# A differential attention head's two maps merged on VectorE ahead of their turning

## The chip, the cores and the metric

One core of a Trainium2 chip runs the whole program in one launch. The metric is the device time of an execution in microseconds, lower is better. The kernel before was run three times.

## What is computed

Two stacks of layers follow each other on 256 latent tokens of width 1024, with 256 context tokens beside them: an even layer (convolution, neighbourhood attention, SwiGLU), an odd layer (window attention and differential attention, then a mixture of 8 experts), and a second model with two more layers. All data are float32. The change lies in the odd layer's differential attention. It has 4 heads. Each has two sets of queries and keys of width 64 and one set of values of width 128:

```
def joint_softmax(parts, extra=None):
    m = parts[0].max(-1, keepdims=True)
    for p in parts[1:]:
        m = jnp.maximum(m, p.max(-1, keepdims=True))
    ...
    es = [jnp.exp(p - m) for p in parts]
    ...
    return [e / den for e in es]

def diff_attend(q, kvs, lam):
    scale = q.shape[-1] ** -0.5
    ss = [jnp.einsum('bhiqd,bhikd->bhiqk', q, k, preferred_element_type=jnp.float32) * scale for k, _ in kvs]
    ps = joint_softmax(ss)
    out = None
    for p, (_, v) in zip(ps, kvs):
        a = (p[:, :, 0] - lam * p[:, :, 1]).astype(v.dtype)
        o = jnp.einsum('bhqk,bhkd->bhqd', a, v)
        out = o if out is None else out + o
    return out
```

Both maps of a head run over the 512 keys of latent and context tokens. The result of a head goes through an RMS norm of its own and then into the output projection.

## The kernel before

The program is written out by hand for each engine; semaphores order the engines against each other, and the position of an instruction in an engine's own program is its order. An attention is a list of items. An item is one softmax map of 128 queries by 512 keys (by fewer in the even and the second model's attentions). For item i these steps follow each other:

- TensorE, `scores`: queries by keys into the PSUM bank `SC[i % 2]` (L1432). A window item adds a mask (L1434).
- VectorE, in `attn_dve`: the negated maximum of each row into `negm` (L1485 and L1486 with a floor for window items, L1488 without).
- ScalarE, `attn_act`: the exponential into `prob[i % 2]` in SBUF, with the row sums into `den` (L1504).
- TensorE: four 128x128 transposes by the identity into the PSUM bank `PT[i % 2]` (L1460). This is the turning of the map.
- VectorE, `take`: the copy of the turned map into `probT[i % 2]` (L1479).
- TensorE, `outputs`: four matmuls of the turned map by the values into the item's PSUM bank (L1445), the product.

TensorE's order is: scores of item i+1, turning of item i, product of item i-1, then what `aside` adds. Two buffers stand at each place, so the scores of item i+1 wait for the exponential of item i-1, and the exponential of item i waits for the turning of item i-2. The names `sem("scores")`, `max_done`, `exp_done`, `prob_turned`, `probT_done` and `out_ready` count these steps, one for an item. `e.link` makes VectorE wait for the end of its own instruction before the next; `e.put` names an instruction and `e.after` waits for a name.

The odd layer's list is `W_ITEMS + D_ITEMS`: 16 window items (0 to 15), then 16 differential items (16 to 31). `diff_items` orders the latter by head, then map, then block of 128 queries:

```
for hd in range(4):
    for i in range(2):
        for t in range(NT):
```

Between the steps of an item VectorE does other work that `odd_every_dve` hangs on item numbers: the arguments of the window heads' sinks at item 16, the window heads' outputs at 17 (`window_out_dve`, L2136 to L2143), their cut into a high and a low part for the projection at 25 and 28 (`cut_x`, L1362 and L1363), and for the first two differential heads the reciprocals and lambda (`diff_shares_dve`), the scaling of both maps' products (`diff_scale_dve`, L2217), their sum (`diff_add_dve`, L2224) and the sums of squares (`diff_squares_dve`, L2229 and L2230) at 26 to 31. The other two heads follow behind the attention in `diff_out_dve`. On TensorE `odd_aside_pe` turns the window outputs at items 20 and 22 (L2158), and ScalarE copies them out two items later (L2173). Behind the attention TensorE goes on with the output projection (L422, L423, L426): a first block of weights, the turning of the first two differential heads' outputs (L2260), a second block, the turning of the other two, and the rest.

Of the kernel before, what the change touches and what calls it, by code (L numbers as in the profile page):

```python
# [20 lines left out]
P = 128  # L21
TOK = 256
# [113 lines left out]
def program(nc, a, out, plan):  # L136
# [1280 lines left out]
    def attn_pe(e, base, items, ready, *deps, turn=None, aside=None):  # L1417

        e.after(*deps)
        last = len(items)  # L1420

# [15 lines left out]
        def outputs(i):  # L1437
            it = items[i]

            e.eng.wait_ge(sem("probT_done"), base + i + 1)  # L1440
            if it.get("o_free"):
                it["o_free"](e)
            kt = it["n"] // P
            for k in range(kt):
                ins = nc.tensor.matmul(it["o"], probT[i % 2][:, k * P:k * P + P], it["v"][k],  # L1445
                                       start=k == 0, stop=k == kt - 1)
            ins.then_inc(sem("out_ready"), 1)

        scores(0)
        for i in range(last):  # L1450
            if i + 1 < last:
                scores(i + 1)

            e.eng.wait_ge(sem("exp_done"), base + i + 1)
            if i >= 2:
                e.eng.wait_ge(sem("probT_done"), base + i - 1)
            if turn:
                turn(e, i)
            for k in range(items[i]["n"] // P):
                ins = nc.tensor.transpose(PT[i % 2][:, k * P:k * P + P], prob[i % 2][:, k * P:k * P + P], ident)  # L1460
            ins.then_inc(sem("prob_turned"), 1)
            if i >= 1:
                outputs(i - 1)
            if aside:
                aside(e, i)
        outputs(last - 1)

    def attn_dve(e, base, items, floor, *deps, every=None):


        e.after(*deps)

        def take(i):

            e.eng.wait_ge(sem("prob_turned"), base + i + 1)
            if i >= 2:
                e.eng.wait_ge(sem("out_ready"), base + i - 1)
            n = items[i]["n"]
            nc.vector.tensor_copy(probT[i % 2][:, 0:n], PT[i % 2][:, 0:n]).then_inc(sem("probT_done"), 1)  # L1479

        for i, it in enumerate(items):
# [8 lines left out]
            if i >= 1:  # L1490
                take(i - 1)
            if every:
                every(i)
        take(len(items) - 1)

    def attn_act(e, base, items, also=None):
        for i, it in enumerate(items):
# [3 lines left out]
            if i >= 2:  # L1501

                e.eng.wait_ge(sem("prob_turned"), base + i - 1)
# [332 lines left out]
    def diff_items():  # L1836
        items = []
        for hd in range(4):
            for i in range(2):
                for t in range(NT):  # L1840
                    half = slice(i * HD, i * HD + HD)
                    v = [pl[:, t_, 1792 + hd * P:1792 + hd * P + P] for t_ in range(NT)] + \
                        [pc[:, t_, 768 + hd * P:768 + hd * P + P] for t_ in range(NT)]
                    items.append(dict(n=2 * TOK, q=qTo[half, 4 + hd, t * P:t * P + P], k=kTo[half, 2 + hd, :],
                                                    adds=[], v=v, o=psum[4 + hd // 2 * 2 + t][:, (2 * (hd % 2) + i) * P:(2 * (hd % 2) + i) * P + P]))
        items[0]["o_free"] = lambda e: e.after("att_w:o")
        return items

# [302 lines left out]
    def odd_aside_pe(e, i):  # L2151

        if i in W_TURNS:
            b = W_TURNS.index(i)
            for k in range(2):
                for t in range(NT):
                    at, c = (2 * b + k) * P, k * TOK + t * P
                    ins = nc.tensor.transpose(PT[(i - 1) % 2][:, c:c + P], hc[:, t, at:at + P], ident)  # L2158
            e.put(ins, f"att_w:oT_ps{b}")

    def odd_turn_pe(e, i):

        if i - 1 in W_TURNS:
            e.after(f"att_w:oT{W_TURNS.index(i - 1)}")

    def odd_also_act(e, i):
# [3 lines left out]
        if i - 2 in W_TURNS:  # L2170
            b = W_TURNS.index(i - 2)
            e.after(f"att_w:oT_ps{b}")
            e.put(nc.scalar.activation(xf[:, 2 * b:2 * b + 2, :].rearrange("p k t -> p (k t)"), PT[(i - 3) % 2][:, :],  # L2173
                                       ACT.Copy), f"att_w:oT{b}")

    def odd_every_dve(e, base):

        def every(i):
            if i == W_END:
                window_sinks_dve(e, base)  # L2180
            if i == W_END + 1:
                window_out_dve(e, base)
            if i in (25, 28):
                cut_x(e, "cat_o", (i // 28,), lambda b: f"att_w:oT{b}")
            if i in (26, 27):
                if i == 26:
# [6 lines left out]
        return every  # L2193

# [4 lines left out]
    def diff_shares_dve(e, base, half):  # L2199

        e.eng.wait_ge(sem("out_ready"), base + D_HALF + 8 * half)
        e.eng.wait_ge(sem("exp_done"), base + D_HALF + 8 * half)
        if half == 0:
            e.after("lam exp")
            e.link(nc.vector.tensor_tensor(lame[:, 0:1], lame[:, 2:3], lame[:, 3:4], ALU.subtract))
            e.link(nc.vector.tensor_scalar(lame[:, 0:1], lame[:, 0:1], -1.0, -LAM_INIT, ALU.mult, ALU.add))
        own = den[:, W_END + 8 * half:W_END + 8 * half + 8]
        e.link(nc.vector.reciprocal(own, own))
        r = own.rearrange("p (h i t) -> p h i t", i=2, t=NT)
        e.link(nc.vector.tensor_scalar(r[:, :, 1, :], r[:, :, 1, :], lame[:, 0:1], None, ALU.mult))  # L2210

    def diff_scale_dve(e, half, t):

        r = den[:, W_END + 8 * half:W_END + 8 * half + 8].rearrange("p (h i t) -> p h i t", i=2, t=NT)
        for i, to in enumerate((diff_head(half, t), diff_other[half][:, t * 2 * P:t * 2 * P + 2 * P])):
# [1729 lines left out]
```

## Time and profile before

| | us |
|---|---|
| runs, median (lowest to highest) | 2788.96 (2783.48 to 2789.22) |
| profiled execution, span | 2787.6 |
| TensorE busy in the span | 2662.0 |
| VectorE, ScalarE, GpSimd busy | 1838.2, 1445.3, 182.9 |

The page gives the profiled execution by its span alone. The median of the runs is 1.4 us above it and the fastest run 4.1 below it. All times within the trace count from the start of the span. The odd layer's attention lies between 850 and 943 us, the differential items from 901. In the clock column 1.00 is TensorE's full 2.4 GHz and 0.50 is 1.2 GHz. A matmul's length in the timeline holds its way through the array, so that starts, and not lengths, tell how fast one follows another.

### The profile page before, as it was taken

The page shows a single profiled execution, that of the slowest core. Times are in us where ns is not written, and L with a number is a line of the kernel's source. Part 1 is how long each engine was busy: PE and PEld are TensorE (multiplying, and loading weights), DVE is VectorE, ACT ScalarE, POOL GpSimd, SP SyncE. Part 2 cuts the span into 40 slices and gives each one's busy share as a digit, 9 for nine tenths or more (in the row PEclk, how much of TensorE's full clock was granted, in tenths as well). Part 3 has the DMA queues.
Part 4 walks back from the last instruction along what each step waited for, and adds up shares of the span by engine and source line. Part 5 has one row for each costly group of instructions (what it writes and reads, how often), then busy time and mean ns, then how long its engine had stood idle before and what let it go on. Part 6 is the DMA issues. An engine that isn't in the chain of part 4 may idle for free.

```text
span 2787.6 us, 33943 instructions
## 1 busy us (share of the span) xinstructions
PE 2662.0 (95%) x12949; PEld 2210.6 (79%) x12949; DVE 1838.2 (66%) x2324; ACT 1445.3 (52%) x2055; POOL 182.9 (7%) x226
## 2 busy tenths in 40 slices
PE   7999899999999889999999899998999999998998
PEld 5777678888886678888888788887788788777787
DVE  6676677787776655557888656588656556546555
ACT  6563354544453344446777445664445545553553
POOL 2011000000050000000000000002100100100100
PEclk9999999999999989999999999999999999999999
DMA  8673166776660056557999546540364655650444
GB/s 299 226 249 117 61 220 233 242 263 225 227 186 31 1 174 199 186 186 257 326 326 329 195 155 222 157 151 1 119 199 166 203 174 178 205 188 4 158 159 143
DMA packets 260767, 511.40 MB, mean 183 GB/s; under 512 B 9769, under 2 KB 40705, under 8 KB 260496
## 3 DMA queue, kind: packets, MB, share of 16 engines
q1 hardware_dynamic: 256576, 498.11, 53.4%
q0 software_dynamic: 4048, 11.36, 1.4%
q8 instruction: 93, 1.52, 0.2%
q14 instruction: 50, 0.41, 0.0%
HBM read 507.33 MB, written 1.05 MB: 182 GB/s over the span
## 4 chain that ended last, share of the span: by engine, by line
PE 86%; DVE 7%; ACT 3%; DMA 2%; issue 2%; POOL 1%; SPq 0%; DVEq 0%; ACTq 0%; POOLq 0%
PE bank L422 23%; PE bank L423 23%; PE bank L426 23%; PE bank L1432 2%; PE bank L1445 2%; DVE h_hid L2856 1%; PE bank L393 1%; PE bank L1460 1%; PE bank L394 1%; PE bank L395 1%; DVE wlo L330 1%; ACT whi L326 1%; PE bank L541 1%; PE bank L1434 1%; PE bank L2420 1%
## 5 line engine op out<-in xcount | busy, mean ns | idle before, releaser
L330 DVE TENSOR_TENSOR wlo<-raw,whi 128x1024 fp32r<-128x1024 f32 (+1 forms) x964 | 1142.9, 1201 | 662.0 <-ACT whi L326 655.8
L326 ACT ACTIVATE whi<-raw 128x1024 fp32r<-128x1024 f32 (+1 forms) x964 | 986.9, 1035 | 782.8 <-PE bank L426 733.7
L422 PE MATMUL bank<-whi,xhi 128*128 128x512 f32 (+2 forms) x2320 | 884.7, 381 | 22.1 <-issue 12.7
L426 PE MATMUL bank<-whi,xlo 128*128 128x512 f32 (+2 forms) x2320 | 874.8, 377 | 0.0
L423 PE MATMUL bank<-wlo,xhi 128*128 128x512 f32 (+2 forms) x2320 | 874.0, 377 | 0.0
L422 PEld LDWEIGHTS bank<-whi,xhi 128*128 128x128 f32 x2320 | 439.6, 190 | 103.1 <-issue 20.3
L426 PEld LDWEIGHTS bank<-whi,xlo 128*128 128x128 f32 x2320 | 438.9, 189 | 77.2
L423 PEld LDWEIGHTS bank<-wlo,xhi 128*128 128x128 f32 x2320 | 439.9, 190 | 74.5 <-issue 0.5
L422 PE MATMUL bank<-whi,f_hhi 128*128 128x512 f32 x496 | 194.0, 391 | 0.0
L426 PE MATMUL bank<-whi,f_hlo 128*128 128x512 f32 x496 | 193.1, 389 | 0.0
L423 PE MATMUL bank<-wlo,f_hhi 128*128 128x512 f32 x496 | 193.1, 389 | 0.0
L1504 ACT ACTIVATE tmp<-bank,negm 128x512 f32<-128x512 f32 (+2 forms) x112 | 60.8, 543 | 135.2 <-DVE negm L1488 101.2
L426 PEld LDWEIGHTS bank<-whi,f_hlo 128*128 128x128 f32 x496 | 93.1, 188 | 19.4
L423 PEld LDWEIGHTS bank<-wlo,f_hhi 128*128 128x128 f32 x496 | 93.2, 188 | 19.0
L422 PEld LDWEIGHTS bank<-whi,f_hhi 128*128 128x128 f32 x496 | 93.1, 188 | 19.0
L422 PE MATMUL bank<-whi,m_hhi 128*128 128x512 f32 x242 | 95.7, 396 | 0.0
L426 PE MATMUL bank<-whi,m_hlo 128*128 128x512 f32 x242 | 94.6, 391 | 0.0
L423 PE MATMUL bank<-wlo,m_hhi 128*128 128x512 f32 x242 | 94.4, 390 | 0.0
L641 DVE TENSOR_TENSOR f_hlo<-bank,f_hhi 128x512 fp32r<-128x512 f32 (+1 forms) x66 | 42.8, 687 | 72.2 <-ACT f_hhi L597 72.0
L597 ACT ACTIVATE f_hhi<-bank 128x512 fp32r<-128x512 f32 (+1 forms) x66 | 36.2, 595 | 82.9 <-PE bank L541 82.9
L1488 DVE TENSOR_REDUCE negm<-bank 128x1 f32<-128x256 f32 (+2 forms) x96 | 45.9, 479 | 49.7 <-PE bank L1434 31.8
L1460 PE MATMUL bank<-kb,tmp 128*128 128x128 f32 x296 | 55.9, 291 | 13.3 <-ACT tmp L1504 11.9
(574 smaller groups left out, 2804.2 us busy)
## 6 DMA issues: line engine op xcount, KB each, us to landing
raw<-in_ffn_w SPq DMA_DIRECT2D x180, 1024.0 KB, 5.1
raw<-in_moe_w SPq DMA_DIRECT2D x96, 1024.0 KB, 6.1
raw<-in_moe_w SPq DMA_DIRECT2D x48, 768.0 KB, 4.6
raw<-in_ada_w SPq DMA_DIRECT2D x24, 1024.0 KB, 5.6
raw<-in_ev_w_in SPq DMA_DIRECT2D x24, 1024.0 KB, 5.6
raw<-in_ffn_w SPq DMA_DIRECT2D x36, 512.0 KB, 3.6
raw<-in_hyb_w_in SPq DMA_DIRECT2D x18, 1024.0 KB, 5.1
raw<-in_attn_w_qkv SPq DMA_DIRECT2D x18, 1024.0 KB, 5.0
```

The source lines that it names most:

```text
L326: nc.scalar.activation(whole, part, ACT.Copy).then_inc(sem("w_hi"), 1)
L330: nc.vector.tensor_tensor(wlo[s][:, 0:rows, 0:n], part, whole.bitcast(F32), ALU.subtract)\
L422: nc.tensor.matmul(bank[:, 0:n], xk_h, whi[s][:, wk, 0:n], start=first, stop=False)
L423: ins = nc.tensor.matmul(bank[:, 0:n], xk_h, wlo[s][:, wk, 0:n], start=False, stop=last and xl is None)
L426: ins = nc.tensor.matmul(bank[:, 0:n], xk_l, whi[s][:, wk, 0:n], start=False, stop=last)
L597: ins = nc.scalar.activation(hhi[:, at, :].rearrange("p k t -> p (k t)"), T[b // TOK][:, 0:k * TOK], ACT.Copy)
L641: ins = nc.vector.tensor_tensor(hlo[:, at, :].rearrange(flat), T[b // TOK][:, 0:k * TOK], hhi[:, at, :].bitcast(F32).rearrange(flat), ALU. ...
L1432: nc_last = nc.tensor.matmul(bank[:, 0:n], it["q"], it["k"], start=True, stop=not adds)
L1445: ins = nc.tensor.matmul(it["o"], probT[i % 2][:, k * P:k * P + P], it["v"][k], start=k == 0, stop=k == kt - 1)
L1460: ins = nc.tensor.transpose(PT[i % 2][:, k * P:k * P + P], prob[i % 2][:, k * P:k * P + P], ident)
L1488: nc.vector.tensor_reduce(col, SC[i % 2][:, 0:it["n"]], AX.X, ALU.max, negate=True)\
L1504: nc.scalar.activation(prob[i % 2][:, 0:it["n"]], SC[i % 2][:, 0:it["n"]], ACT.Exp, bias=negm[:, i:i + 1], accum_out=den[:, i:i + 1]).then ...
```

## The change

The two maps of a head and block of queries now follow each other: the first is called `lead`, the second `pair`. VectorE merges them before they are turned: the second map is multiplied by c = -lambda x (sum of the first) / (sum of the second), and the first is added. One turning, one copy and one product serve both. The sum of the first map divides the product at the end, as before. `turned_items` numbers the items that are turned, and the banks `PT` and buffers `probT` alternate by this number, which starts at `tb`; in the odd layer 24 of 32 items are turned. The products of four heads and two blocks take two PSUM banks in place of four. The window outputs are turned into banks 6 and 7, so `odd_turn_pe` goes.

```
     def attn_pe(...)
+        def turn_over(i):
+            u = place[i]
+            if items[i].get("pair"):
+                e.after(f"merged{i}")
+            else:
+                e.eng.wait_ge(sem("exp_done"), base + i + 1)
+            if u >= 2:
+                e.eng.wait_ge(sem("probT_done"), tb + u - 1)
...
+            for k in range(items[i]["n"] // P):
+                ins = nc.tensor.transpose(PT[u % 2][:, k * P:k * P + P], prob[i % 2][:, k * P:k * P + P], ident)
+            ins.then_inc(sem("prob_turned"), 1)
...
+            now = i
+            if items[i].get("lead"):
+                now = i - 1 if i and items[i - 1].get("pair") else None
+            elif items[i].get("pair"):
+                now = "later"
+            if now != "later":
+                if now is not None:
+                    turn_over(now)
+                if waiting is not None:
+                    outputs(waiting)
+                waiting = now
     def attn_dve(...)
             if i >= 1:
-                take(i - 1)
+                former = items[i - 1]
+                if former.get("pair"):
+                    former["merge"](e, i - 1)
+                elif not former.get("lead"):
+                    take(i - 1)
+                elif i >= 2 and items[i - 2].get("pair"):
+                    take(i - 2)
     def attn_act(...)
             if i >= 2:
-
-                e.eng.wait_ge(sem("prob_turned"), base + i - 1)
+                if items[i - 2].get("lead"):
+
+                    e.after(f"merged{i - 1}")
+                else:
+                    e.eng.wait_ge(sem("prob_turned"), tb + place[i - 2] + 1)
+    def diff_merge_dve(e, i):
+
+        e.eng.wait_ge(sem("exp_done"), ATT0[2] + i + 1)
+        c = vtop[:, (i - W_END) // 2:(i - W_END) // 2 + 1]
+        e.link(nc.vector.reciprocal(c, den[:, i:i + 1]))
+        e.link(nc.vector.scalar_tensor_tensor(out=c, in0=c, scalar=lame[:, 0:1], in1=den[:, i - 1:i],
+                                              op0=ALU.mult, op1=ALU.mult))
+        own, other = prob[(i - 1) % 2], prob[i % 2]
+        e.put(nc.vector.scalar_tensor_tensor(out=other[:, :], in0=other[:, :], scalar=c, in1=own[:, :],
+                                             op0=ALU.mult, op1=ALU.add), f"merged{i}")
     odd_aside_pe
         if i in W_TURNS:
             b = W_TURNS.index(i)
+            e.after("att_w:o")
...
     odd_every_dve
             if i == W_END:
                 window_sinks_dve(e, base)
+                lambda_total_dve(e)
...
-            if i in (25, 28):
-                cut_x(e, "cat_o", (i // 28,), lambda b: f"att_w:oT{b}")
-            if i in (26, 27):
-                if i == 26:
+            if i in (25, 27):
+                cut_x(e, "cat_o", (i // 27,), lambda b: f"att_w:oT{b}")
+            if i in (28, 29):
+                if i == 28:
                     diff_shares_dve(e, base, 0)
-                diff_scale_dve(e, 0, i - 26)
-            if i == 29:
-                diff_add_dve(e, 0)
+                diff_scale_dve(e, 0, i - 28)
```

`diff_scale_dve` scales one product for a block in place of two, `diff_add_dve` goes in both halves, and `diff_shares_dve` no longer computes lambda, which `lambda_total_dve` does at item 16 with the same two instructions. In the second model's attention only the numbers change (`TURNED4 = 56`).

How the order moves. On TensorE, in the differential part of the odd attention, a little over two items before (o_kT is the keys, `kb` the identity, tmp the maps and turned maps, o_pl and o_pc the values of latent and context):

```order
L1432 MATMUL bank<-o_kT,o_qT 128x512
L1460 MATMUL bank<-kb,tmp 128x128 x4
L1445 MATMUL bank<-o_pl,tmp 128x128 x2
L1445 MATMUL bank<-o_pc,tmp 128x128 x2
L1432 MATMUL bank<-o_kT,o_qT 128x512
```

and now a little over one pair:

```order
L1438 MATMUL bank<-o_kT,o_qT 128x512 x2
L1466 MATMUL bank<-kb,tmp 128x128 x4
L1451 MATMUL bank<-o_pl,tmp 128x128 x2
L1451 MATMUL bank<-o_pc,tmp 128x128 x2
L1438 MATMUL bank<-o_kT,o_qT 128x512 x2
```

A turning and a product stood behind the scores of each item; now they stand behind the scores of two. The turning is that of the pair before, the product that of the pair before it.

On VectorE, from the maximum of item 17 over the window heads' outputs to item 18, before:

```order
L1488 TENSOR_REDUCE negm<-bank 128x1
L1479 COPY tmp<-bank 128x512
L2136 TENSOR_TENSOR den<-den,sinke 128x16
L2137 RECIPROCAL den<-den 128x16
L2143 TENSOR_TENSOR hc<-bank,den 128x256 x4
L1488 TENSOR_REDUCE negm<-bank 128x1
```

and now:

```order
L1517 TENSOR_REDUCE negm<-bank 128x1
L2195 TENSOR_TENSOR den<-den,sinke 128x16
L2196 RECIPROCAL den<-den 128x16
L2202 TENSOR_TENSOR hc<-bank,den 128x256 x4
L1517 TENSOR_REDUCE negm<-bank 128x1
L1901 RECIPROCAL vtop<-den 128x1
L1902 SCALAR_TENSOR_TENSOR vtop<-vtop,few,den 128x1
L1905 SCALAR_TENSOR_TENSOR tmp<-tmp,vtop 128x512
L1517 TENSOR_REDUCE negm<-bank 128x1
L1508 COPY tmp<-bank 128x512
```

Behind the maximum of item 17 stood the copy of item 16; item 16 now has none. Behind the maximum of item 18 stands the first merge (L1901, L1902, L1905), and behind that of item 19 the copy of the merged map.

At the end of the attention on VectorE, before:

```order
L2229 TENSOR_TENSOR y<-hc 128x256
L2230 TENSOR_REDUCE ss<-y 128x2
L1488 TENSOR_REDUCE negm<-bank 128x1
L1479 COPY tmp<-bank 128x512
L2229 TENSOR_TENSOR y<-hc 128x256
L2230 TENSOR_REDUCE ss<-y 128x2
L1479 COPY tmp<-bank 128x512
```

and now:

```order
L2274 TENSOR_TENSOR y<-hc 128x256
L2275 TENSOR_REDUCE ss<-y 128x2
L1517 TENSOR_REDUCE negm<-bank 128x1
L1508 COPY tmp<-bank 128x512
L2274 TENSOR_TENSOR y<-hc 128x256
L2275 TENSOR_REDUCE ss<-y 128x2
L1901 RECIPROCAL vtop<-den 128x1
L1902 SCALAR_TENSOR_TENSOR vtop<-vtop,few,den 128x1
L1905 SCALAR_TENSOR_TENSOR tmp<-tmp,vtop 128x512
L1508 COPY tmp<-bank 128x512
```

The last merge stands behind both rounds of squares, and the last copy directly behind that merge.

## Rows read from the trace of the kernel before

**Rows 1.** Page, parts 1 and 4: busy time, and the chain that ended last.
```profile
PE 2662.0 (95%) x12949; PEld 2210.6 (79%) x12949; DVE 1838.2 (66%) x2324; ACT 1445.3 (52%) x2055; POOL 182.9 (7%) x226
...
PE 86%; DVE 7%; ACT 3%; DMA 2%; issue 2%; POOL 1%; SPq 0%; DVEq 0%; ACTq 0%; POOLq 0%
```

**Rows 2.** Windows: start:end, length, busy PE, PEld, DVE, ACT, POOL, granted clock, DMA share, GB/s.
```profile
899.40:942.20 42.80, 41.99 (x243) 28.30 (x242) 29.93 (x58) 13.77 (x35) 0.61 (x2) 1.00 0.00 1
```

**Rows 3.** Timeline, TensorE, maps 16 and 17: start, length, instruction group.
```profile
900.84 1.12 PE L1432 MATMUL bank<-o_kT,o_qT 64*128 64x512 f32 x2
901.89 0.66 PE L1460 MATMUL bank<-kb,tmp 128*128 128x128 f32 x4
902.39 0.61 PE L1445 MATMUL bank<-o_pl,tmp 128*128 128x128 f32 x4
...
903.37 1.12 PE L1432 MATMUL bank<-o_kT,o_qT 64*128 64x512 f32 x2
904.43 0.66 PE L1460 MATMUL bank<-kb,tmp 128*128 128x128 f32 x4
```

**Rows 4.** Timeline, VectorE, the same stretch.
```profile
902.07 0.69 DVE L1488 TENSOR_REDUCE negm<-bank 128x1 f32<-128x512 f32 x1 [1.23 <-PE bank L1432]
902.68 0.68 DVE L1479 COPY tmp<-bank 128x512 f32<-128x512 f32 x1
903.27 0.17 DVE L2136 TENSOR_TENSOR den<-den,sinke 128x16 f32<-128x16 f32 x1
...
905.59 0.69 DVE L1488 TENSOR_REDUCE negm<-bank 128x1 f32<-128x512 f32 x1
```

**Rows 5.** Timeline, all engines, the end of the last map.
```profile
939.99 0.69 ACT L1504 ACTIVATE tmp<-bank,negm 128x512 f32<-128x512 f32 x1 [1.76 <-DVE negm L1488]
...
940.82 0.42 PEld L1460 LDWEIGHTS bank<-kb,tmp 128*128 128x128 f32 x4 [0.37 <-ACT tmp L1504]
...
941.57 0.69 DVE L1479 COPY tmp<-bank 128x512 f32<-128x512 f32 x1 [0.23 <-PE bank L1460]
...
942.32 0.52 PEld L1445 LDWEIGHTS bank<-o_pl,tmp 128*128 128x128 f32 x4
...
943.23 0.48 PE L422 MATMUL bank<-whi,xhi 128*128 128x512 f32 x1
```

**Rows 6.** Groups by line and form, VectorE: count, busy us, mean ns.
```profile
L2693 DVE SCALAR_TENSOR_TENSOR h<-y,ss,h 128x512 f32<-128x512 f32 x24 | 18.0, 750 | 3.4 <-POOL ss L2712 3.1
...
L1355 DVE SCALAR_TENSOR_TENSOR scal<-mod,cols 128x4 f32<-128x4 f32 x4 | 0.7, 164 | 0.1
...
L2208 DVE RECIPROCAL den<-den 128x8 f32<-128x8 f32 x2 | 0.4, 203 | 0.1
...
L2217 DVE TENSOR_TENSOR hc<-bank,den 128x256 f32<-128x256 f32 x4 | 1.7, 422 | 0.1
```

**Rows 7.** Timeline, TensorE: turning of the second half's head outputs.
```profile
954.71 0.60 PE L2260 MATMUL bank<-kb,hc 128*128 128x128 f32 x4
```

**Rows 8.** Timeline, VectorE: the last scaling of head outputs.
```profile
952.19 0.88 DVE L2237 TENSOR_TENSOR hc<-hc,ss 128x256 f32<-128x256 f32 x2 [0.90 <-POOL ss L824]
```

**Rows 9.** Windows: stretches with idle time of TensorE, and those behind them.
```profile
2009.80:2013.20 3.40, 1.44 (x9) 0.99 (x10) 2.80 (x7) 3.28 (x12) 0.74 (x2) 1.00 0.27 102
2013.20:2016.60 3.40, 3.40 (x9) 2.66 (x10) 3.37 (x9) 3.02 (x8) 0.22 (x1) 0.50 0.00 0
...
852.60:856.10 3.50, 1.61 (x7) 0.90 (x7) 2.60 (x7) 2.22 (x6) 0.00 (x0) 1.00 0.00 0
856.10:866.30 10.20, 10.20 (x31) 6.69 (x30) 3.43 (x7) 1.56 (x4) 0.00 (x0) 0.50 0.00 0
...
316.70:330.40 13.70, 10.51 (x64) 7.34 (x64) 13.17 (x29) 9.64 (x25) 2.19 (x4) 1.00 0.09 16
```

**Rows 10.** Timeline, TensorE at a granted clock of 0.50: scores, turning.
```profile
860.45 2.07 PE L1432 MATMUL bank<-o_kT,o_qT 64*128 64x512 f32 x2
...
862.83 1.05 PE L1460 MATMUL bank<-kb,tmp 128*128 128x128 f32 x4
```

More of the change, by code:

```diff
@@ L1415, in program, with turned_items, attn_pe @@
     ITEM = Count()
-    def attn_pe(e, base, items, ready, *deps, turn=None, aside=None):
+    def turned_items(items):
+        return {i: u for u, i in enumerate(i for i, it in enumerate(items) if not it.get("lead"))}
+    def attn_pe(e, base, items, ready, *deps, turn=None, aside=None, tb=None):
         e.after(*deps)
         last = len(items)
+        tb = base if tb is None else tb
+        place = turned_items(items)
         def scores(i):
@@ L1437, in outputs @@
         def outputs(i):
[L1438 to L1440 removed]
+            it, u = items[i], place[i]
+            e.eng.wait_ge(sem("probT_done"), tb + u + 1)
             if it.get("o_free"):
@@ L1490, in attn_dve, with attn_act @@
             if i >= 1:
-                take(i - 1)
+                former = items[i - 1]
[5 more added lines that the diff above has]
+                    take(i - 2)
             if every:
                 every(i)
+        if items[-1].get("pair"):
+            items[-1]["merge"](e, len(items) - 1)
         take(len(items) - 1)
-    def attn_act(e, base, items, also=None):
+    def attn_act(e, base, items, also=None, tb=None):
+        tb = base if tb is None else tb
+        place = turned_items(items)
         for i, it in enumerate(items):
@@ L1838, in diff_items @@
         for hd in range(4):
-            for i in range(2):
-                for t in range(NT):
+            v = [pl[:, t_, 1792 + hd * P:1792 + hd * P + P] for t_ in range(NT)] + \
+                [pc[:, t_, 768 + hd * P:768 + hd * P + P] for t_ in range(NT)]
+            for t in range(NT):
+                for i in range(2):
                     half = slice(i * HD, i * HD + HD)
[L1842 to L1846, printed above, removed]
-        return items
+                    it = dict(n=2 * TOK, q=qTo[half, 4 + hd, t * P:t * P + P], k=kTo[half, 2 + hd, :], adds=[])
+                    if i == 0:
+                        it["lead"] = True
+                    else:
+                        it.update(pair=True, v=v, merge=diff_merge_dve,
+                                  o=psum[4 + hd // 2][:, (2 * t + hd % 2) * P:(2 * t + hd % 2) * P + P])
+                    items.append(it)
+        items[1]["o_free"] = lambda e: e.after("att_w:o")
+        return items
+    def diff_merge_dve(e, i):
[7 more added lines that the diff above has]
+                                             op0=ALU.mult, op1=ALU.add), f"merged{i}")
     def odd_pool(e):
@@ L2172, in odd_also_act @@
             e.after(f"att_w:oT_ps{b}")
-            e.put(nc.scalar.activation(xf[:, 2 * b:2 * b + 2, :].rearrange("p k t -> p (k t)"), PT[(i - 3) % 2][:, :],
-                                       ACT.Copy), f"att_w:oT{b}")
+            e.put(nc.scalar.activation(xf[:, 2 * b:2 * b + 2, :].rearrange("p k t -> p (k t)"), psum[6 + b][:, :], ACT.Copy),
+                  f"att_w:oT{b}")
     def odd_every_dve(e, base):
```

79 lines of the change are left out of this document (34 added, 45 removed).

## The prediction

> **What bounds the kernel now.** I read the page first. TensorE is busy for 95% of the span and carries 86% of the chain that ended last [rows 1], so a change pays only where it shortens what TensorE does or waits for. Then the busy time by stretch: the 16 maps of the differential heads lie in a stretch of 42.8 us at full clock, in which TensorE is busy for 41.99 us and VectorE for 29.93 [rows 2]. The timeline of TensorE shows the cycle [rows 3]: scores of the next map at 900.84, turning of this one at 901.89, product of the one before at 902.39, next scores at 903.37. That is 1.05 + 0.50 + 0.98 = 2.53 us for a map and 5.07 for a pair, without a gap. VectorE's reduction and copy take 0.69 us each and start 0.61 apart [rows 4]. Both end while TensorE is on something else, so the stage is bound by TensorE. It ends at 943.23, when the output projection starts [rows 5].
>
> **What the change takes from TensorE.** Eight of the 16 turnings and eight of the 16 products go: 8 x (0.50 + 0.98) = 11.8 us. The scores stay. Were TensorE still the bound, a pair would take 2 x 1.05 + 0.50 + 0.98 = 3.58 us.
>
> **What the new waits make of it.** The exponential of the next leading map writes over the buffer that the merge reads, so it waits for the merge. Two scores further on TensorE waits for that exponential; VectorE reduces those scores and only behind this issues the next merge. That is a ring, and I price one lap of it, from the end of a merge to the end of the next:
> - The merge's end to a waiting TensorE: 0.06 us, as from VectorE's copy (941.57 + 0.69) to the product at 942.32 [rows 5].
> - The turning and the product of the former pair stand ahead of the scores in TensorE's order: 0.50 + 0.98 [rows 3]. The exponential runs beside them: 0.04 + 0.83 us (939.99 to 940.82, [rows 5]) is less than 1.54.
> - Scores to the start of their reduction: 1.23 us (900.84 to 902.07); the next instruction on VectorE 0.61 later [rows 3, 4].
> - The merge itself. No row of before shows it. Its nearest are a SCALAR_TENSOR_TENSOR on 128x512 that reads and writes SBUF alone, with 750 ns, one on 128x4 with 164 ns and a reciprocal on 128x8 with 203 ns [rows 6]. The first is of the very size; for each of the two small ones I take 0.20 with the gap behind it. Sum 1.15 us; bounds 1.08 and 1.3.
>
> The lap is 0.06 + 0.50 + 0.98 + 1.23 + 0.61 + 0.40 + 0.75 = **4.53 us** against 5.07 now: of the 1.48 us that TensorE saves in a pair, 0.95 becomes a wait.
>
> **The whole stage.** Up to the reduction of map 17 (902.07) nothing differs. Then:
> - VectorE no longer copies map 16 and so is at the window's outputs at 902.68. They take 2.32 us (903.27 to 905.59 now, [rows 4]), hence 905.00. Reduction of map 18: 905.61. First merge done: 906.76. First turning 906.82; the turning of map 17 now starts at 904.43.
> - First lap, with no product in it: 0.04 + 0.83 + 1.23 + 0.61 + 1.15 = 3.86, to 910.68.
> - Two laps with the window outputs' turnings on TensorE: 2 x (4.53 + 0.49) = 10.04, to 920.72. Three plain laps: 13.59, to 934.31.
> - The last lap is VectorE's. Two rounds of squares and sums lie ahead of the last merge. Each has two instructions on 256 columns, which I take at 0.455 with the gap from the 0.42 of today's scaling by the shares, also on 256 columns [rows 6]. It is free at 934.31 - 0.06 - 0.14 = 934.11 (the next instruction starts 0.14 before a wide one ends: 0.61 against 0.75). From there 0.91 + 0.61 + 0.61 + 0.91 + 1.15 = 4.19, and 0.06 to the last turning: 938.36.
> - From the last turning to the projection is 2.41 us now (940.82 to 943.23, [rows 5]) and has the same steps afterwards: 940.77.
>
> That is **2.5 us** earlier than 943.23. Laps that are 0.1 us off in either direction make it 1.8 or 3.2.
>
> **What I cost at nothing.** The two small instructions on lambda move to map 16, where VectorE waits over 1 us for scores [rows 4]. In each full lap VectorE has 0.61 + 1.15 + 0.61 + 0.61 = 2.98 us of ring work, so about 1.5 us free. Each cut of x (1.1), share with scale (0.7) or round of squares (0.9) fits, except at the end as counted. If that cover went, each would cost at most its own length, once. Behind the attention VectorE has fewer scales, no additions and no second map for either half, about 2.1 us less. But the last turning of head outputs starts at 954.71 while its input is ready at 952.19 + 0.88 = 953.07 [rows 7, 8], so TensorE's order sets that part already and nothing comes of it. No DMA is issued, moved or passed by the change; the loads stand still in the stage (DMA share 0.00, [rows 2]) and shift with it. The third and fourth attention only count from other numbers.
>
> **The clock.** TensorE will now stand idle, which it does not today: some 1.8 us before the first turning (the second scores end near 905.0), 0.9 in each lap and 2.6 before the last turning (935.8 to 938.4). In this trace a stretch in which it was busy for 1.61 of 3.50 us, with one wait of 1.9, is followed by 10.2 us at a granted clock of 0.50, that is 1.2 GHz in place of 2.4; another, busy for 1.44 of 3.40, by 3.4 us at 0.50 [rows 9]. Elsewhere it was busy for 10.51 of 13.70 us and stayed at 1.00 [rows 9], which is 77% and near the 3.58 of 4.53 (79%) of my laps. So I expect the laps at 2.4 GHz and one fall at the end, as likely as not, with dense work behind it: 3.4 us at half speed cost 1.7. Between the ends 0 and 1.7 I take 0.9, the middle: the wait is longer than the one of 1.9 that led to a fall, but two cases are no rule. The Trainium skill ("TensorE: Matmul & The Clock Gate", "A second HAM failure mode: psum-queue depth-cycling") says that frequent short idle spells between groups of matmuls make the gate swing between half and full clock. By that rule the laps would not stay at full clock, which is the second rival. The trace disagrees so far, by the 13.70 us just named.
>
> **Sum.** -2.5 + 0.9 = -1.6 us on a span of 2787.6. The median of the three runs is 2788.96, 1.4 above that span, and I carry the difference over to it: **2787.4 us**. A measurement of this kernel tells about 0.2% (5.6 us) from no change, so this is "no difference".
>
> **Rivals.**
> 1. *The merge is hidden* (faster). If ScalarE ran a pair ahead and the ring did not bind, a pair would take 3.58 us: -11.8, back 2.4 for the first turning and 2.4 for the last lap: -7.0, or 2782.0. For it speaks that VectorE has a third of the stage free [rows 2]. Against it speaks that there are two buffers of maps: the exponential of a pair's first map cannot start before the merge has read the buffer. Chance 0.10.
> 2. *The clock falls in the laps* (slower). At 0.50 scores show 2.07 us and a turning 1.05 [rows 10] against 1.12 and 0.66 [rows 3]; the product I put at its 0.98 in the proportion of the turning, +0.58. That is 0.95 + 0.39 + 0.58 = +1.9 us in a lap. Two such laps cost what the stage gains; four of them with the fall at the end give -2.5 + 7.6 + 1.7 = +6.8, or 2795.8, which is where this begins to count as slower; all eight give +14.4, or 2803.4. For it: the 1.8 us gap before the first turning has nearly the length of the wait that led to 10.2 us at 0.50, and the scores of 64 rows that are the same in both places follow. Against it: the busy stretch at 77%. Chance 0.07.
> 3. *The laps are longer than priced*, by 0.35 us each, through slower small instructions, or a squares or cut step that does land in the ring: seven laps give back 2.5 us. With the 0.9 of the clock that is 2789.9. Chance 0.13.
> 4. *The change does not do what it says*: if the removed turnings were issued all the same, the ring would be on top and the stage longer. The order shows them gone, so this gets no chance of its own.
>
> That leaves 0.70 for the forecast. The range 2782.5 to 2791.5 takes in the forecast with its bounds, rival 3, the scatter of 5.7 us that the three runs have, and the slow edge of the first rival; the second is left out. Faster by over 0.2% needs 2783.4 or less: rival 1 and a tail of the forecast by scatter, 0.13. Slower by over 0.2%: rival 2 and a little of rival 3, 0.08. The rest, 0.79, is the same.
>
> **What would show it.** In the trace after: turnings of the merged maps 4.5 us apart (5.0 at the two with the window outputs' turnings), the first near 906.8 and the last near 938.4; the wide merge instruction at 0.75 us; TensorE idle for about 0.9 us before each turning, put down to the merge, and for about 2.6 before the last; the projection's start near 940.8 if all before it stands where it stood. Laps of 3.6 us would make rival 1 right, a granted clock of 0.50 inside the laps rival 2. If the stage is 2.5 us shorter and the whole is not, the rest is clock or scatter elsewhere. The forecast is wrong if the stage itself changes by under 1 or over 4 us.

## The result and the profile after

The changed kernel takes 2796.76 us (median of 5 runs, 2795.78 to 2798.00) against 2788.96 before (5 runs, 2783.48 to 2791.00). The medians lie 7.8 us apart, the means 9.5. The ratio is 1.0034 with a 95% interval of 1.0022 to 1.0046: **slower by about 0.3%**. The forecast was 2787.4 and "no difference". It was wrong, and the second rival, the one on the slow side, is what happened.

Times in the odd attention are counted from here on from the start of the maximum of map 17 (902.07 before, 898.23 after), up to which the attention's instructions stand in the same order, to the first matmul of the output projection. (From the first scores to that maximum it is 51.64 us before and 49.41 after, with 10.2 and 6.8 us of it at 0.50.) I call this the stage. It took 41.16 us before and takes 46.63 after. The predicted value was 38.7.

The page of the changed kernel, parts 1 and 4:

```profile
PE 2658.5 (95%) x12853; PEld 2210.0 (79%) x12853; DVE 1837.3 (66%) x2330; ACT 1445.3 (52%) x2055; POOL 180.1 (6%) x226
...
PE 84%; DVE 7%; ACT 3%; DMA 3%; issue 2%; POOL 1%; SPq 0%; ACTq 0%; DVEq 0%; POOLq 0%
```

TensorE has 96 matmul records fewer [rows 1] and its busy time hardly falls, by 3.5 us where the prediction took away 11.8, which is the first sign: what it still does takes longer.

Windows of the changed kernel (start:end, length, busy time of PE, PEld, DVE, ACT, POOL, granted clock, DMA share, GB/s):

```profile
898.20:944.80 46.60, 32.73 (x139) 21.61 (x140) 30.88 (x66) 12.75 (x32) 1.23 (x2) 0.74 0.00 1
900.96:903.00 2.04, 0.00 (x0) 0.00 (x0) 1.94 (x6) 0.00 (x0) 0.00 (x0) 1.00 0.00 0
903.40:913.60 10.20, 8.98 (x27) 4.81 (x25) 3.91 (x9) 3.36 (x9) 0.00 (x0) 0.50 0.00 0
913.60:920.50 6.90, 3.19 (x21) 2.20 (x22) 4.92 (x11) 2.20 (x6) 0.00 (x0) 0.99 0.00 0
```

Against [rows 2] the granted clock over the stage is 0.74 and not 1.00. The wait before the first turning (second line) is followed at once by 10.2 us at 1.2 GHz. In the fourth line the clock is full, and there TensorE is busy for 3.19 of 6.90 us; that window holds two waits and the work of one lap. Later come more stretches at 0.50. With the first it is 23.9 us in all.

Timeline of TensorE, changed kernel (start, length, group, idle time before it and what ended it); L1438 are scores, L1466 turnings:

```profile
899.14 1.82 PE L1438 MATMUL bank<-o_kT,o_qT 64*128 64x512 f32 x4
903.01 0.78 PE L1466 MATMUL bank<-kb,tmp 128*128 128x128 f32 x4 [2.05 <-DVE tmp L1905]
...
911.46 2.08 PE L1438 MATMUL bank<-o_kT,o_qT 64*128 64x512 f32 x4
915.42 0.66 PE L1466 MATMUL bank<-kb,tmp 128*128 128x128 f32 x4 [1.89 <-DVE tmp L1905]
...
917.34 1.13 PE L1438 MATMUL bank<-o_kT,o_qT 64*128 64x512 f32 x4
920.35 1.04 PE L1466 MATMUL bank<-kb,tmp 128*128 128x128 f32 x4 [1.89 <-DVE tmp L1905]
...
941.14 1.12 PE L1466 MATMUL bank<-kb,tmp 128*128 128x128 f32 x4 [1.76 <-DVE tmp L1905]
...
944.86 0.48 PE L422 MATMUL bank<-whi,xhi 128*128 128x512 f32 x1
```

Two things stand here. The waits for the merge (L1905) are 1.89 us in most laps, twice the 0.95 that I had reckoned with. And the scores of *both* maps of a pair, four records, take 1.13 us at full clock (917.34); a single map's two records took 1.12 in [rows 3]. The first records of the two maps start at 917.338 and 917.344. The merge itself is as priced (VectorE's timeline, changed kernel: maximum, reciprocal, small product, merge):

```profile
918.50 0.69 DVE L1517 TENSOR_REDUCE negm<-bank 128x1 f32<-128x512 f32 x1 [1.69 <-PE bank L1438]
919.11 0.15 DVE L1901 RECIPROCAL vtop<-den 128x1 f32<-128x1 f32 x1
919.29 0.22 DVE L1902 SCALAR_TENSOR_TENSOR vtop<-vtop,few,den 128x1 f32<-128x1 f32 x1
919.55 0.75 DVE L1905 SCALAR_TENSOR_TENSOR tmp<-tmp,vtop 128x512 f32<-128x512 f32 x1
```

From 919.11 to the end at 920.30 it is 1.19 us against 1.15. The lap at full clock from the turning at 915.42 to that at 920.35, with the window outputs' turning in it, is 4.93 against 4.53 + 0.49 = 5.02. So the ring is right where the clock is full. What makes the stage long is then its pace at 1.2 GHz, which the runs below test. The turnings' starts are 4.8, 9.6, 17.2, 22.1, 28.2, 34.2, 38.8 and 42.9 us into the stage.

### The profile page after: what moved, and what is told of

Read it like the earlier page. It is cut to its first block, busy times and chain, and to the rows that moved or that the text cites. A ratio compares the mean times of both kernels' runs of the same rounds, so it can differ in the third digit from the quotient of the medians.

```text
span 2794.0 us, 33741 instructions
## 1 busy us (share of the span) xinstructions
PE 2658.5 (95%) x12853; PEld 2210.0 (79%) x12853; DVE 1837.3 (66%) x2330; ACT 1445.3 (52%) x2055; POOL 180.1 (6%) x226
## 3 DMA queue, kind: packets, MB, share of 16 engines
HBM read 507.33 MB, written 1.05 MB: 182 GB/s over the span
## 4 chain that ended last, share of the span: by engine, by line
PE 84%; DVE 7%; ACT 3%; DMA 3%; issue 2%; POOL 1%; SPq 0%; ACTq 0%; DVEq 0%; POOLq 0%
PE bank L422 23%; PE bank L423 23%; PE bank L426 22%; PE bank L1438 2%; PE bank L1451 2%; DVE h_hid L2900 1%; PE bank L393 1%; DMA raw<-in_moe_w 1%; ACT whi L326 1%; PE bank L395 1%; PE bank L394 1%; PE bank L1466 1%; DVE wlo L330 1%; PE bank L541 1%; PE bank L1440 1%
## 5 line engine op out<-in xcount | busy, mean ns | idle before, releaser
L326 ACT ACTIVATE whi<-raw 128x1024 fp32r<-128x1024 f32 (+1 forms) x964 | 987.1, 1036 | 787.6 <-PE bank L426 733.9
L1466 PE MATMUL bank<-kb,tmp 128*128 128x128 f32 x264 | 52.8, 302 | 25.6 <-DVE tmp L1905 13.8
```

Of the source, the lines that this page charges most:

```text
L326: nc.scalar.activation(whole, part, ACT.Copy).then_inc(sem("w_hi"), 1)
L1466: ins = nc.tensor.transpose(PT[u % 2][:, k * P:k * P + P], prob[i % 2][:, k * P:k * P + P], ident)
```

## The experiments

Theory 1: TensorE idles in each lap, the clock falls for that reason, and the stage loses more at 1.2 GHz than the merge saves. Theory 2: the ring is longer than priced, or VectorE's total counts, and the clock is an accident. All runs that follow are compared with runs of the kernel before on the same chip: r0 to r3 on one, r4 to r7 on a second, r8 to r11 on a third. "Stage" is each one's profiled execution. L1907, L1908 and L1550 are the merge and the exponential in the edited kernels.

**r0, the changed kernel again.** No edit.

> The changed kernel once more, as the base of the next three. Every theory: 0.2 to 0.45% slower than before; the differential part starts with a wait of TensorE of about 2.0 us, has waits of 1.9 us before each turning where the clock is full, and 0.50 granted in part of it. If the falls of the clock come from these waits, the stage holds 15 to 30 us at 0.50 again, though at other places; if they were a matter of that one execution, the stage is free of them and 2.5 us shorter than before.

Measured: 2800.88 us, ratio 1.0053 (1.0040 to 1.0066). Stage 49.08 us, 33.4 us of it at 0.50. The falls are not an accident of one execution. The first begins again directly behind the first turning and lasts 10.2 us. The first turnings stand at 4.79, 9.63, 17.20, 22.14 and 28.25, as in the other trace to 0.02 us.

**r1, the waits filled.** Before each turning of a merged map TensorE turns the identity into the bank that the turning then overwrites:

```
+            if u >= 2:
+                e.eng.wait_ge(sem("probT_done"), tb + u - 1)
             if items[i].get("pair"):
+                for _ in range({17: 18, 31: 22}.get(i, 15)):
+                    nc.tensor.transpose(PT[u % 2][:, 0:P], ident, ident)
                 e.after(f"merged{i}")
             else:
                 e.eng.wait_ge(sem("exp_done"), base + i + 1)
-            if u >= 2:
-                e.eng.wait_ge(sem("probT_done"), tb + u - 1)
```

> The changed kernel with needless transposes of the identity ahead of each turning of a merged map (18 before the first, 22 before the last, 15 else, about 0.11 us each), written into the bank that the turning then overwrites. They fill most of TensorE's wait for the merge, and lengthen nothing that waits. Theory 1 (the loss is the clock's, which falls because TensorE stands idle): no 0.50 in the stage, laps of about 4.5 us (5.0 at two), projection 2 to 3 us earlier than before counted from the scores of map 17, time 0.2 to 0.4% below the changed kernel. Theory 2 (the ring of waits itself is longer than priced, the clock matters little): laps stay above 5 us and the time stays within 0.1% of the changed kernel.

Measured: 2787.12 us, ratio 1.0002 (0.9992 to 1.0013), 0.5% below r0. Window of the whole stage and TensorE's timeline (L1461 are the needless transposes, L1468 the turnings):

```profile
898.90:937.80 38.90, 38.48 (x269) 29.56 (x269) 30.87 (x66) 12.62 (x32) 1.23 (x2) 1.00 0.00 1
```

```profile
910.90 1.86 PE L1461 MATMUL bank<-kb 128*128 128x128 f32 x15
912.86 0.66 PE L1468 MATMUL bank<-kb,tmp 128*128 128x128 f32 x4
...
915.83 1.86 PE L1461 MATMUL bank<-kb 128*128 128x128 f32 x15
917.79 0.66 PE L1468 MATMUL bank<-kb,tmp 128*128 128x128 f32 x4
...
922.29 0.66 PE L1468 MATMUL bank<-kb,tmp 128*128 128x128 f32 x4
...
937.85 0.47 PE L422 MATMUL bank<-whi,xhi 128*128 128x512 f32 x1
```

With 130 more matmuls in the program the clock stays at 1.00 and the stage takes 38.99 us: 2.2 us less than before, where the prediction said 2.5. The laps are 4.93 and 4.50 (predicted 5.02 and 4.53). All the instructions and all the waits of the change are there; only TensorE's idle time is gone. That shows theory 1 for the stage, and with it the ring.

**r5, only the long waits filled.** As r1 with `{17: 18, 31: 22}.get(i, 0)`.

> The changed kernel with needless transposes before the first and the last turning only (18 and 22), none in the laps. If it is the two long waits alone that make the clock fall: no 0.50 in the laps, stage as in the run with filler everywhere (39.0 us from the maximum of map 17 to the projection), time 0.4% below the changed kernel. If the 1.9 us waits of every lap do it on their own: 0.50 in several laps, 42 to 47 us, time within 0.2% of the changed kernel. I expect the second.

Measured: 2798.24 us, ratio 1.0028 (1.0014 to 1.0042). TensorE's timeline and the window of the stage:

```profile
914.52 0.63 PE L1468 MATMUL bank<-kb,tmp 128*128 128x128 f32 x4 [1.98 <-DVE tmp L1907]
...
921.14 0.63 PE L1468 MATMUL bank<-kb,tmp 128*128 128x128 f32 x4 [1.99 <-DVE tmp L1907]
```

```profile
899.10:945.60 46.50, 35.13 (x179) 25.00 (x180) 30.90 (x66) 12.80 (x32) 1.22 (x2) 0.82 0.00 1
```

The stage holds 17.1 us at 0.50, in five stretches of 3.4 us, and takes 46.51 us: the waits of every lap do it on their own. The 10.2 us that lay directly behind the first turning are gone now that its wait is filled; the first fall comes at 908.4, one lap later. So the first wait has its fall too, but filling it and the last one does not save the stage.

**r6, the waits half filled.** As r1 with 8 transposes in a lap.

> As the run with filler everywhere, but 8 transposes in a lap in place of 15. That leaves TensorE about 1.0 us idle in a lap of 4.5, which is the idle time that the prediction had reckoned with (0.9). If the prediction's reading of the clock was right and only its idle time was too small: no 0.50 in the laps and 39 to 40 us from the maximum of map 17 to the projection. If also 1.0 us is too much: falls as in the changed kernel, 42 us or more.

Measured: 2783.11 us, ratio 0.9973 (0.9964 to 0.9983).

```profile
915.79 0.66 PE L1468 MATMUL bank<-kb,tmp 128*128 128x128 f32 x4 [0.87 <-DVE tmp L1907]
917.27 1.23 PE L1438 MATMUL bank<-o_kT,o_qT 64*128 64x512 f32 x4
920.29 0.66 PE L1468 MATMUL bank<-kb,tmp 128*128 128x128 f32 x4 [0.77 <-DVE tmp L1907]
```

```profile
897.20:935.80 38.60, 34.45 (x227) 25.03 (x228) 30.90 (x66) 12.56 (x32) 1.23 (x2) 1.00 0.00 1
```

With waits of 0.8 to 0.9 us in the laps, about those that the prediction had drawn, the clock stays full and the stage is 38.61 us, 2.55 less than before and as predicted to 0.1. So the prediction's reading of the clock held for the laps with the idle time it assumed. The idle time was wrong. r6 says nothing on the waits before the first and the last turning, which it fills with 18 and 22 transposes as r1 does.

**r7, one matmul more.** r6 with the scores of each pair's second map issued twice:

```
-            nc_last = nc.tensor.matmul(bank[:, 0:n], it["q"], it["k"], start=True, stop=not adds)
+            for _ in range(2 if it.get("pair") else 1):
+                nc_last = nc.tensor.matmul(bank[:, 0:n], it["q"], it["k"], start=True, stop=not adds)
```

> As the run before, with the scores of each pair's second map issued twice, one behind the other, into the same bank. The two maps of a pair read queries and keys from different halves of the partitions, 64 rows each. Theory A (two matmuls of 64 rows from different halves run beside each other in TensorE, two of the same half one behind the other): the group of scores takes about 1.13 us at full clock for the two different ones and 2.2 with the third. Theory B (64-row scores at that place are faster for another reason, such as the bank or their being issued back to back): three take about 1.7 us. The ring is not touched by either.

```profile
911.49 1.99 PE L1439 MATMUL bank<-o_kT,o_qT 64*128 64x512 f32 x6
```

Three take 1.99 us where two of different halves take 1.13. The third, of the same half as the second, adds 0.86; the second, of the other half than the first, added 0.01. That lies between theory A's 2.2 and B's 1.7, nearer to A. The two records of the third start 0.43 us apart, so 0.86 is its full length in a dense row: it runs behind the second and not beside it. That the two maps of a pair do run beside each other stands in their starts. That the different halves are the reason is not separated from one rival: the third matmul also writes the bank of the second, while the two maps of a pair write different banks. Different banks alone are not enough for matmuls of 128 rows, since a product's start stands 0.50 us behind the turning's in [rows 3]; for 64 rows no run has the same half with different banks. One execution; it took 2790.87 us with a stage of 39.78, which I read nothing from.

**r2, the merge ahead of the maximum.** In `attn_dve`:

```
         for i, it in enumerate(items):
+            if i >= 1 and items[i - 1].get("pair"):
+                items[i - 1]["merge"](e, i - 1)
             e.eng.wait_ge(sem("scores"), base + i + 1)
...
                 if former.get("pair"):
-                    former["merge"](e, i - 1)
+                    pass
```

> The changed kernel with one thing moved: on VectorE the merge of a pair stands ahead of the maximum of the next map and not behind it. That takes the scores of the next pair out of the ring. Theory 1: the ring is then merge 1.2, maximum and exponential of both maps, 3.45 us in all; TensorE has 2.6 us of work in it and idles 0.8, too little for the clock to fall; the stage ends 6 to 8 us earlier than before counted from the scores of map 17, and the time is 0.15 to 0.3% below before and 0.5% below the changed kernel. If the clock falls also at 0.8 us of idle in 3.45: laps of 4 to 4.5 us and a time near before. Theory 2 (no ring, VectorE's total is what counts): within 0.1% of the changed kernel, since not one instruction less is issued.

Measured: 2784.54 us, ratio 0.9989 (0.9980 to 0.9999), 0.6% below r0. Stage 37.47 us: 3.7 less than before, not 6 to 8. Laps in the undisturbed part are 3.97 us against 3.45, and two stretches at 0.50 remain (11.8 us), each behind a longer wait: before the first turning with the scores behind it, and before the last turning. It refutes theory 2 for the changed kernel, since the same instructions in another order give 11.6 us in the stage. In the laps of 3.97 us VectorE goes without a gap: they hold a cut of x of 1.1 us, which the 3.45 had left out. So with the merge ahead VectorE's total has begun to count.

**r3, side work moved too.** Besides, the second half of the window heads' outputs goes behind the maximum of map 18, and the last `diff_squares_dve` of the first half behind the last merge.

```
         if items[-1].get("pair"):
             items[-1]["merge"](e, len(items) - 1)
+            diff_squares_dve(e, 0, 1)
...
+            if i == W_END + 2:
+                window_part_dve(e, 1)
...
-            if i in (30, 31):
-                diff_squares_dve(e, 0, i - 30)
+            if i == 30:
+                diff_squares_dve(e, 0, 0)
```

> As the run before, and two more pieces of VectorE's side work off the path: half of the window heads' outputs behind the first merge and the next maximum, and the last round of squares behind the last merge. Expected: first turning 0.9 us earlier, last one 1 to 2 us earlier than in the run before, time 0 to 0.1% below it.

Measured: 2785.82 us, ratio 0.9998 (0.9987 to 1.0008). Stage 36.38 us. The first turning is 0.92 us earlier than in r2, as expected. The last is 0.6 earlier, less than expected. The time did not follow: these runs cannot tell r3 from r2, nor r3 from before. Timeline of TensorE, with the waits that are left:

```profile
901.80 0.66 PE L1466 MATMUL bank<-kb,tmp 128*128 128x128 f32 x4 [0.54 <-DVE tmp L1908]
903.21 3.58 PE L1438 MATMUL bank<-o_kT,o_qT 64*128 64x512 f32 x4 [0.76 <-ACT tmp L1550]
...
931.20 1.11 PE L1466 MATMUL bank<-kb,tmp 128*128 128x128 f32 x4 [2.62 <-DVE tmp L1908]
```

The scores at 903.21 take 3.58 us. Part of it is a wait, since the second map's scores start only at 904.73 behind an exponential; at full clock, in r11 below, the same stretch takes 2.64. The rest is the clock, which has fallen again (0.50 from 903.67).

**r4 and r11, r3 with its waits filled** (`{17: 5, 21: 0, 23: 0, 29: 2, 31: 20}.get(i, 6)` transposes).

> The third variant (merge ahead of the maximum, half of the window outputs and the last squares behind) with needless transposes of the identity in TensorE's remaining waits: 5 before the first turning, 20 before the last, 0 to 6 else. Theory 1 (what was lost there is again the clock: 10 us at 0.50 in the stage): no 0.50 in the stage, laps of 4.0 us or less, projection 33 to 34 us after the maximum of map 17 (41.16 before, 36.38 in that variant), time 0.1 to 0.3% below before. Rival (the falls in that variant come from the window part or the warm-up before): 0.50 again in the same places.

> The late variant with needless transposes once more, as the base of the warm start. Stage 8 us shorter than before, 0.997 to 0.998 of before as at the first time.

Measured: 2783.61 us, 0.9975 (0.9965 to 0.9985), and 2781.69 us, 0.9981 (0.9970 to 0.9992). Both stages are free of falls and take 33.05 and 33.03 us, 8.1 less than before. Window of the stage in r4:

```profile
899.60:932.60 33.00, 31.11 (x184) 20.99 (x185) 29.82 (x65) 12.31 (x32) 1.22 (x2) 1.00 0.00 1
```

VectorE is now busy for 29.82 of 33.00 us, and in r11 it has no gap of over 0.15 us from 913 to 928.9 us: over most of the laps it has become what sets the pace.

**r9 and r10, r1 and r6 again** on one chip.

> The run with 15 needless transposes in each lap once more, beside the next two on one chip. It came out at 1.0002 of before although its stage was 2.2 us shorter, while the run with 8 came out at 0.9973 with a stage 2.5 us shorter. If the scatter of the clock elsewhere is the reason, both give 0.998 to 1.000 now.

> The run with 8 needless transposes in each lap once more. Stage 2.5 us shorter than before; 0.998 to 1.000 of before if the first figure was helped by scatter, 0.997 again if not.

Measured: r9 2788.26 us, 1.0006 (0.9997 to 1.0015); r10 2785.90 us, 0.9994 (0.9984 to 1.0003). Stages 38.97 and 38.59 us, equal to the first ones within 0.02. The 0.9973 of r6 did not come again: the stage repeats, the ratio moved by more than its interval. So an interval here covers the runs of one chip, and not the step from one to the next. 15 transposes come out slower than 8 both times, by more than the 0.4 us between the stages; r1 and r6 ran on different chips, and the intervals of r9 and r10 overlap. In the profiled executions most of the rest lies behind the attention: the stretch from the projection to the experts' weights (bounded as under "The whole" below) takes 117.7 and 120.1 us with 15 (30.7 and 34.1 us of it at 0.50) and 115.6 and 117.5 with 8 (23.9 and 30.7). Why is not shown.

**r8, a wait that was always there.** r4 with 16 transposes more ahead of the turning of item 0, where TensorE waits 1.9 us for the first exponential in every kernel here, before included.

```
+            if i == 0 and items[-1].get("pair"):
+                e.after("dlT")
+                for _ in range(16):
+                    nc.tensor.transpose(psum[6][:, 0:P], ident, ident)
```

> The late variant with needless transposes (merge ahead of the maximum, side work moved, waits filled), and 16 more of them in a wait that the kernel before has as well: 1.9 us ahead of the turning of item 0, behind which all traces so far show 3.4 to 10.2 us at 0.50. Expected: no 0.50 between 845 and the projection; the time from there to the maximum of map 17 shorter by 2 to 4 us than in the other runs; time 0.05 to 0.15% below the late variant with needless transposes and 0.3 to 0.45% below before. If the clock was not what made the first window items slow, no difference to that variant.

Measured: **2779.74 us** (2775.99 to 2780.94), ratio 0.9971 (0.9961 to 0.9981). It is the fastest kernel of the study, ahead of both given ones. Window and timeline of r8 (the stretch of the window items, then the needless transposes and item 0's turning):

```profile
845.00:898.00 53.00, 52.88 (x289) 35.12 (x288) 32.19 (x66) 19.91 (x47) 0.00 (x0) 1.00 0.00 1
898.00:931.00 33.00, 31.12 (x178) 21.89 (x179) 28.32 (x61) 11.64 (x30) 1.22 (x2) 0.95 0.00 1
```

```profile
851.06 1.91 PE L1479 MATMUL bank<-kb 128*128 128x128 f32 x16
853.09 0.66 PE L1468 MATMUL bank<-kb,tmp 128*128 128x128 f32 x4
```

From the first scores to the maximum of map 17 it takes 46.83 us against 49.35 in r11, 2.5 less. In [rows 9] that wait was followed by 10.2 us at 0.50; here by none. One stretch of 3.4 us at 0.50 came back in the stage, against the expectation, 3.7 us behind the first merged turning, and made the stage 34.64 us. r4 and r11 have the same waits of 0.75 and 0.40 us there and no fall, so what brought it is open.

## Why the prediction was wrong

**The bound and the saved work: right as far as they went.** Eight turnings and eight products are gone, and the stage was TensorE's before.

**The step that failed: "The scores stay", with 2 x 1.05 us for a pair, and from it an idle time of 0.95 us in a lap that is 79% busy.** The change puts the two maps of a head next to each other. One reads queries and keys in rows 0 to 63 of the partitions, the other in rows 64 to 127, and TensorE does both in the time of one: 1.13 us in place of 2.1. The work left in a lap is 0.50 + 0.98 + 1.13 = 2.61 us and not 3.58. Since the ring never waited for the second scores, none of the 1.0 us became time. All of it became idle time: 1.89 us in a lap and not 0.95. The kernel before never shows scores of different halves one behind the other, but the diff and the slice `half` did say that they would be. The Trainium skill ("TensorEngine Tiling (Array Packing)", "Key Properties") says that different tiles of the array can load weights and multiply in parallel. The trace agrees, with 0.01 us for the second map's scores and 0.86 for a third matmul of the same half (r7; it shares the bank too). I had read the 64 rows in the trace and not asked which.

**The clock: right for the laps as drawn, applied to the wrong lap, and one wait put at nothing.** I compared 79% with a stretch that was busy for 77% at full clock. At the assumed idle time the clock does stay full in the laps (r6: waits of 0.77 and 0.87 us). At the real one it falls within the laps alone (r5). The comparison was by shares; by the length of the waits it was thinner, since the timeline of that stretch of before has none over 0.65 us. And the clock's term in the sum, +0.9 us, priced a fall at the end only. The prediction listed 1.8 us of idle time before the first turning as well and gave it no price, though its own [rows 9] have a wait of 1.9 us followed by 10.2 us at 0.50. Measured were 2.05 us and 10.2 us at 0.50 behind them, in both traces of the changed kernel; at the third turning the first of these traces is already 3.6 us behind r6, of 8.0 over the stage. No run has the prediction's waits in all three places, so what the forecast's own idle times would have cost stays open.

The prediction drew on the Trainium skill ("TensorE: Matmul & The Clock Gate", "A second HAM failure mode: psum-queue depth-cycling"), where frequent short idle spells between groups of matmuls make the gate swing. The trace agrees at waits of 1.9 us and more: 0.50 from 903.4, 920.5, 927.3 and 937.5, full clock between. At waits of 0.8 to 0.9 us (r6, r10) it does not. Taken as a warning it deserved more than the 0.07 that the second rival got.

**The ring: right.** Predicted from rows of before were laps of 4.53 and 5.02 us, a first turning 4.75 into the stage and a stage of 38.7. Measured where the clock is full (r1, r6): 4.50, 4.93, 4.79, and 39.0 and 38.6. The merge had 1.15 for 1.19.

**The second rival: right in kind, near in size.** It priced a cold lap at +1.9 us and said that four would make the change slower. Against r1 and r6 the stage lost 7.6 to 8.0 us in the first trace and 10.1 to 10.5 in r0. That is four to five and a half such laps. With the 7.8 between r1 and r6, -2.5 + 7.8 = +5.3 in the stage; measured +5.5.

**The whole.** The stage is not all of the loss. The span of the profiled execution is 6.4 us above before. The stage has 5.5 of it, the window items ahead of it -2.2, and 4.1 lie in the stretch behind the attention, from the start of the projection to one and the same ScalarE instruction (L326, a conversion of the experts' weights, at 1059.12 and 1064.82); the remainder is -0.9. In r0, 11.5 us above before, it is 7.9, -3.2, 2.8 and 4.0. The windows of the stretch, before and then after:

```profile
943.23:1059.12 115.89, 96.80 (x467) 82.51 (x466) 68.59 (x125) 46.52 (x63) 5.43 (x6) 0.90 0.38 125
944.86:1064.82 119.96, 101.39 (x467) 87.04 (x466) 66.35 (x118) 46.41 (x64) 3.54 (x6) 0.86 0.37 121
```

TensorE is at 0.50 for 23.9 us of it before and for 34.1 after. r4, r8 and r11 have the same 34.1 us in the same 120 us and have lower medians than before all the same, by what they save ahead of it. r6 has 23.9 us in 115.6, and r10, the same kernel, 30.7 in 117.5. So this part changes from execution to execution, and one trace of before cannot tell whether the change made it longer.

More generally, the rest of the span outside the stage lies between 2741.7 and 2756.4 us over all the profiles (before: 2746.4) and goes with the time at 0.50 in it, by about 0.46 us for each us (correlation 0.89 over the 14 traces): 111.4 us at 0.50 in r8, which is the lowest, 124.4 in before, 134.8 in the changed kernel, 142.1 in r4 and r5, which are the highest. Those two were profiled in their slowest execution. What holds the clock down longer there in one execution than in another stays open. The scatter of a kernel is also wider than the 5.7 us that the prediction took from three runs: 90 later runs of the kernel before, on three chips, lie between 2779.6 and 2795.8 us, and the slower ones have the lower mean clock (correlation -0.86).

## What to carry to other kernels

Taking work off the engine that sets the pace is worth only what the next chain of waits leaves of it; when that engine is TensorE, the rest is idle time that can cost its clock, and then more can be lost than was saved. So work out the share of idle time in the new lap before trusting the gain, from what the matmuls will take in their *new* neighbourhood. If a wait can't be shortened by putting the instruction that others wait for (here the merge) ahead of work that nobody waits for yet, a few needless matmuls in it are cheap: r1 gave back 0.5% against r0. They must end before the wait does. In r1 the 15 ahead of the second turning, in the one lap without a product, make it 0.44 us later than the 8 of r6.

## What the hardware showed that I had not expected

- Two matmuls of 64 rows from different halves of the partitions and into different banks, issued one behind the other, take 1.13 us together; one takes 1.12. A third one of the second's half and bank adds 0.86 us.
- 15 transposes of 128 columns in a 1.9 us wait hold the granted clock at 1.00 where without them it went to 0.50 in the laps (r1 and r9 against r0 and r5); 8 of them, leaving 0.8 to 0.9 us idle, do as well (r6 and r10).
- The kernel before has such a place too, a wait of 1.9 us ahead of its first turning. 16 transposes in it, tried in the late variant (r8 against r11), took 2.5 us off the window items behind it. Their time goes with the time at 0.50 in them: 46.83 us with none, 48.43 with 3.4 us (r6), 49.41 with 6.8 (the changed kernel), 51.64 with 10.2 (before).
- The same instructions in another order on VectorE (r2 against r0) changed the stage from 49.1 to 37.5 us.
